# Memory's keys and values as 512-column products with a VectorE join, and the norms' transposes in the accumulating banks

## The reference, cut to what matters

```
def _memory_attention(q, mem, w_kv):                 # w_kv: 1024 x 512, one per layer
    km, vm = jnp.split(mem @ w_kv, 2, axis=-1)       # keys and values, 256 tokens x 256 each
    ...
    logits = jnp.einsum('bshd,bmhd->bhsm', q, km)
    probs = jax.nn.softmax(logits, axis=-1)
    return jnp.einsum('bhsm,bmhd->bshd', probs, vm)

for layer in range(DEPTH):
    p = x @ w_in                                     # mixer's inputs and memory's queries
    y = concatenate([mixed, recalled]) @ w_o[layer]
    x = _layer_norm(ALPHA * x + y, ...)
    x = _layer_norm(ALPHA * x + _conv_ffn(x, ...), ...)
```

## Time and profile before

| | |
|---|---|
| median of 3 runs | 1253.87 us (1253.64 to 1254.35) |
| span of the profiled execution, first to last instruction | 1251.8 us |
| TensorE busy, its mean granted clock | 1242.1 us (99%), 0.998 |
| VectorE busy | 1023.4 us (82%) |
| ScalarE busy | 729.7 us (58%) |
| KM products, 3 x 64 | L766, L767, L768 on memory |
| VM products, 3 x 64 | L791, L793, L795 on memory |

### The profile page before, as it was taken

The page is one execution under the profiler, slowest core; times in us unless marked ns, Lnnn a source line. Parts: engine busy times, 40 slices in busy tenths (PEclk is TensorE's granted clock), DMA queues, the critical chain, the costliest instruction groups (busy, mean ns, idle before and its releaser), DMA issues.

```text
span 1251.8 us, 19743 instructions
## 1 busy us (share of the span) xinstructions
PE 1242.1 (99%) x7408; PEld 1088.8 (87%) x7408; DVE 1023.4 (82%) x1596; ACT 729.7 (58%) x1187; POOL 20.0 (2%) x29
## 2 busy tenths in 40 slices
PE   8999999999999999999999999999999999999997
PEld 7898888888999998888888888888888888888886
DVE  5776888888879888988888878988888776888887
ACT  5666665555676545655554545655554674755552
POOL 0000000000000000000000000000000000000000
PEclk9999999999999999999999999999999999999999
DMA  9634475555453345666655665665555533666561
GB/s 329 223 120 146 169 249 182 189 188 193 161 184 122 129 140 167 220 202 188 192 189 170 211 209 172 221 200 187 190 193 171 187 118 119 212 209 202 191 193 54
DMA packets 63530, 228.23 MB, mean 182 GB/s; under 512 B 7462, under 2 KB 9126, under 8 KB 62412
## 3 DMA queue, kind: packets, MB, share of 16 engines
q1 hardware_dynamic: 63436, 226.97, 55.1%
HBM read 225.88 MB, written 1.06 MB: 181 GB/s over the span
## 4 chain that ended last, share of the span: by engine, by line
PE 99%; DVE 0%; issue 0%; DVEq 0%
PE pair L734 28%; PE acc L828 21%; PE pair L737 14%; PE pair L766 4%; PE pair L767 4%; PE pair L768 4%; PE acc L734 2%; PE acc L809 2%; PE acc L807 2%; PE acc L808 2%; PE pair L996 2%; PE pair L791 1%; PE pair L795 1%; PE pair L793 1%; PE acc L907 1%; PE acc L737 1%
## 5 line engine op out<-in xcount | busy, mean ns | idle before, releaser
L1253 DVE TENSOR_TENSOR w_lo<-raw,w_hi 128x1024 fp32r<-128x1024 f32 x403 | 485.9, 1220 | 109.8 <-ACT w_hi L1019 108.3
L1019 ACT ACTIVATE w_hi<-raw 128x1024 fp32r<-128x1024 f32 x403 | 423.7, 1058 | 213.7 <-PE pair L737 71.6
L734 PE MATMUL pair<-xT,w_hi 128*128 128x512 f32 x1520 | 478.0, 396 | 0.0
L737 PEld LDWEIGHTS pair<-xT,w_lo 128*128 128x128 f32 x1520 | 285.5, 188 | 67.1
L737 PE MATMUL pair<-xT,w_lo 128*128 128x256 f32 x1520 | 298.7, 278 | 0.0
L734 PEld LDWEIGHTS pair<-xT,w_hi 128*128 128x128 f32 x1520 | 233.8, 189 | 3.1 <-issue 0.3
L1066 ACT ACTIVATE hid<-pair 128x512 f32<-128x512 f32 x88 | 52.6, 597 | 126.0 <-PE pair L737 126.0
L766 PE MATMUL pair<-xT,w_hi 128*128 128x256 f32 x352 | 102.5, 291 | 0.0
L1294 DVE TENSOR_TENSOR hid<-pair,hid 128x512 f32<-128x512 f32 x88 | 60.6, 689 | 48.0 <-ACT hid L1066 47.6
L767 PE MATMUL pair<-xT,w_hi 128*128 128x256 f32 x352 | 99.5, 283 | 0.0
L768 PE MATMUL pair<-xT,w_lo 128*128 128x256 f32 x352 | 99.5, 283 | 0.0
(11 more groups left out here) (219 smaller groups left out, 1668.5 us busy)
## 6 DMA issues: line engine op xcount, KB each, us to landing
raw<-in_stream SPq DMA_DIRECT2D x404, 512.0 KB, 4.6
gains<-in_ln SPq DMA_DIRECT2D x8, 1024.0 KB, 8.5
bias<-bias_scratch SPq DMA_DIRECT2D x2, 1152.0 KB, 9.1
y_tok<-in_mem SPq DMA_DIRECT2D x1, 1024.0 KB, 11.1
out<-x_tok SPq DMA_DIRECT2D x4, 256.0 KB, 2.0
x_tok<-in_x SPq DMA_DIRECT2D x1, 512.0 KB, 3.7
x_tok<-in_x SPq DMA_DIRECT2D x2, 256.0 KB, 4.9
masks_in<-in_masks_c SPq DMA_DIRECT2D x1, 512.0 KB, 8.4
```

The lines of the kernel that those rows point to most:

```text
L734: pe.matmul(bank, w_hi[:, slot, kk * P:(kk + 1) * P], xT[:, kk].rearrange("p a s -> p (a s)"), start=(kk == 0), stop=(kk == KT - 1), skip_ ...
L737: last = pe.matmul(bank[:, 0:SEQ], w_lo[:, slot, kk * P:(kk + 1) * P], xT[:, kk, 0, :], start=False, stop=(kk == KT - 1), skip_group_check ...
L1019: nc.scalar.activation(w_hi[:, u % SPLIT, :], raw[:, u % RAW, :], ACT.Copy).then_inc(hi_ready, 1)
L1253: v.tensor_tensor(w_lo[:, u % SPLIT, :], raw[:, u % RAW, :], w_hi[:, u % SPLIT, :].bitcast(F32), ALU.subtract).then_inc(lo_ready, 1)
```

## The change

1. KM becomes wide: it reads the memory in one tile `memT` with the parts side by side, as x has it, and uses both banks of its pair. The "begun" first half of its second unit, used in the close, moves to the wide code.
2. VM becomes wide with the roles exchanged: memory is the weight, and 512 columns are the high and the low part of the streamed weights. These now lie in one tile `w_split`, high and low part of a slot one after the other. Two k of 512-column products are followed by two of 256.
3. ScalarE copies the upper halves (`mem_lower`), VectorE adds the lower ones (`join`) and only then are keys or values ready. The join is pending work like the taps: it stands behind the first half of the next chunk. Pending work is now put ahead of a chunk's `between` items.
4. All transposes of norms go to ACC: tile 0 to ACC 0 and 1, tile 1 to ACC 2 and 3.

```
-    LATER = {"UA": "taps", "UB": "taps"}
+    LATER = {"UA": "taps", "UB": "taps", "KM": "join", "VM": "join"}
...
         items.append(("half", c, 0))
         if levels:
             round_early(2 * c + 1 + AHEAD)
-        items.extend(between)
         items.extend(late)
         late.clear()
+        items.extend(between)
...
             if following:
 
+                late.append(("join", c + 1))
                 chunks.append(following)
...
+    mem_wide = {c for c, ch in enumerate(chunks) if ch[1] in ("KM", "VM")}
...
-    EARLY_TURNS = {(m, 1) for m in range(2 * DEPTH - 1)}
+    EARLY_TURNS = {(m, t) for m in range(2 * DEPTH - 1) for t in range(TT)}
...
-                chunks[item[1]][1] in ("UA", "UB") or item[1] in xq_wide | qk_wide):
+                chunks[item[1]][1] in ("UA", "UB") or item[1] in xq_wide | qk_wide | mem_wide):
             banks = (proj_ord[item[1]] % 2,)
...
-        w_hi = sb("w_hi", [P, SPLIT, UNIT], F32R)
-        w_lo = sb("w_lo", [P, SPLIT, UNIT], F32R)
+        w_split = sb("w_split", [P, SPLIT, 2, UNIT], F32R)
+        w_hi, w_lo = w_split[:, :, 0, :], w_split[:, :, 1, :]
...
-            return ACC[b] if items[pos][1:3] in EARLY_TURNS else side_bank(pos, b)
+            return ACC[2 * items[pos][2] + b] if items[pos][1:3] in EARLY_TURNS else side_bank(pos, b)
...
-                elif role in ("UA", "UB") or c in conv_wide | xq_wide | qk_wide:
+                elif role in ("UA", "UB", "KM") or c in conv_wide | xq_wide | qk_wide:
...
+                    of = memT if role == "KM" else xT
+                    first, end = (0, KT // 2) if begun else (KT // 2 if i == 1 and c in parted else 0, KT)
+                    for k in range(first, end, 2):
...
+                elif role == "VM":
+
+                    if i == 0:
+                        side(pos)
+                    for t in [0] if begun else [1] if i == 1 and c in parted else [0, 1]:
+                        bank, tok = PAIR[proj_ord[c] % 2][:, t, :], slice(t * P, (t + 1) * P)
+                        for j in range(0, 4, 2):
+                            for jj in (j, j + 1):
+                                pe.matmul(bank.rearrange("p (a e) -> p a e", a=2), a_hi(4 * i + jj, tok),
+                                          w_split[:, slot, :, jj * 256:(jj + 1) * 256], start=(i == 0 and jj == 0), stop=(i == 1 and jj == 3),
+                                          skip_group_check=True)
+                            for jj in (j, j + 1):
+                                last = pe.matmul(bank[:, 0:256], a_lo(4 * i + jj, tok), w_hi[:, slot, jj * 256:(jj + 1) * 256],
+                                                 start=False, stop=(i == 1 and jj == 3), skip_group_check=True)
...
+                elif c in mem_wide:
+                    nc.scalar.activation(km[:] if role == "KM" else vm[:], PAIR[n % 2][:, :, SEQ:512], ACT.Copy).then_inc(mem_lower, 1)
...
+            def join(c):
+                to, ready = (km, km_ready) if chunks[c][1] == "KM" else (vm, vm_ready)
+                dve.wait_ge(mem_lower, sorted(mem_wide).index(c) + 1)
+                v.tensor_tensor(to[:], PAIR[proj_ord[c] % 2][:, :, 0:SEQ], to[:], ALU.add).then_inc(ready, 1)
```

More of the change, by code:

```diff
@@ L339, in trunk_kernel @@
         raw = sb("raw", [P, RAW, UNIT])
-        w_hi = sb("w_hi", [P, SPLIT, UNIT], F32R)
-        w_lo = sb("w_lo", [P, SPLIT, UNIT], F32R)
+        w_split = sb("w_split", [P, SPLIT, 2, UNIT], F32R)
+        w_hi, w_lo = w_split[:, :, 0, :], w_split[:, :, 1, :]
         xT = sb("xT", [P, KT, 2, SEQ], F32R)
         xT_hi, xT_lo = xT[:, :, 0, :], xT[:, :, 1, :]
-        memT_hi = sb("memT_hi", [P, KT, SEQ], F32R)
-        memT_lo = sb("memT_lo", [P, KT, SEQ], F32R)
+        memT = sb("memT", [P, KT, 2, SEQ], F32R)
+        memT_hi, memT_lo = memT[:, :, 0, :], memT[:, :, 1, :]
         mixT_hi = sb("mixT_hi", [P, KT, SEQ], F32R)
@@ L475, in trunk_kernel @@
         rows_done, rows_ready = sem("rows_done"), sem("rows_ready")
-        xq_lower, qk_lower = sem("xq_lower"), sem("qk_lower")
+        xq_lower, qk_lower, mem_lower = sem("xq_lower"), sem("qk_lower"), sem("mem_lower")
         xq_ready, km_ready, vm_ready = sem("xq_ready"), sem("km_ready"), sem("vm_ready")
@@ L728, in half @@
                             side(pos)
-                    for k in range(0, KT, 2):
-                        if i == 0 and k == KT // 2:
+                    of = memT if role == "KM" else xT
+                    first, end = (0, KT // 2) if begun else (KT // 2 if i == 1 and c in parted else 0, KT)
+                    for k in range(first, end, 2):
+                        if i == 0 and k == KT // 2 and role != "KM":
                             pe.wait_ge(turn_lo, xT_turned)
                         for kk in range(k, k + 2):
-                            pe.matmul(bank, w_hi[:, slot, kk * P:(kk + 1) * P], xT[:, kk].rearrange("p a s -> p (a s)"),
+                            pe.matmul(bank, w_hi[:, slot, kk * P:(kk + 1) * P], of[:, kk].rearrange("p a s -> p (a s)"),
                                       start=(kk == 0), stop=(kk == KT - 1), skip_group_check=True)
                         for kk in range(k, k + 2):
-                            last = pe.matmul(bank[:, 0:SEQ], w_lo[:, slot, kk * P:(kk + 1) * P], xT[:, kk, 0, :],
+                            last = pe.matmul(bank[:, 0:SEQ], w_lo[:, slot, kk * P:(kk + 1) * P], of[:, kk, 0, :],
                                              start=False, stop=(kk == KT - 1), skip_group_check=True)
@@ L760, in half @@
                     every = slice(0, SEQ)
-                    first, end = (0, KT // 2) if begun else (KT // 2 if i == 1 and c in parted else 0, KT)
-                    for k in range(first, end):
+                    for k in range(KT):
                         at = slice(k * P, (k + 1) * P)
-                        if i == 0 and k == KT // 2 and role != "KM":
+                        if i == 0 and k == KT // 2:
                             pe.wait_ge(turn_lo, xT_turned)
@@ L781, in half @@
                             last.then_inc(value_done, 1)
+                elif role == "VM":
[11 more added lines that the diff above has]
+                                                 start=False, stop=(i == 1 and jj == 3), skip_group_check=True)
                 elif form == "T":
                     bank = PROJ[proj_ord[c] % 2]
-                    for t in [0] if begun else [1] if i == 1 and c in parted else [0, 1]:
+                    for t in range(TT):
                         dst, tok = bank[:, t * 256:(t + 1) * 256], slice(t * P, (t + 1) * P)
@@ L1417, in _ @@
                     outer_taps(item[1])
+                elif name == "join":
+                    join(item[1])
                 elif name == "q0":
```

## The result

| | before | changed |
|---|---|---|
| median | 1253.91 us (1253.64 to 1254.35, 5 runs) | 1258.39 us (1258.26 to 1258.77, 5 runs) |
| ratio | | 1.0038, 95% interval 1.0027 to 1.0048 |
| span of the profiled execution | 1251.8 us | 1256.5 us |

The account below looks back on a forecast made before the run. TensorE, busy 1242.1 of 1251.8 us, was taken as the bound, with VectorE costing only where TensorE waits. Layer 0 +2.1 and six closes +2.1 gave +4.2 us: span 1256.0, median 1258.1; range 1254.5 to 1260.3.

Parts of the forecast that it names:

- Products, -11.5 ns per k: Keys and values chunks: wide products take 348 ns per k instead of 360; 1.5 us less over 128 units.
- Layer 0, bias rows, +0.78: Layer 0's keys chunk start: first product waits for ScalarE's copy of the bias rows from its bank; +0.78 us.
- Layer 0, memory logits and third query-key chunk, together with the bias rows +2.1: Layer 0: both wait for joins behind weight roundings; logits +1.32, chunk +2.12 us including the earlier delays.
- The idle times: Layer 0, changed profile: TensorE idle about 0.8 us before the memory logits and 0.8 before the third query-key chunk.
- Six closes, +2.1: Ends of half layers: TensorE waits for joins queued behind roundings; 0.34 us at three with keys, 0.36 at three with values.
- release read from one row: TensorE's start after a wait on VectorE: weight load 0.06 us after VectorE's end, part of 0.18 us per wait.
- TensorE would be there at 140.20: Close with keys: the FFN's second chunk could start at 140.20 with the 0.18 us gain, but the join allows 140.72.
- pure-gain rival: Closes and layer 0: joins end early enough, no wait comes, only -1.5 us remains, 1252.4; chance 7%.
- Transposes, 0: Norms: moving transposes to accumulating banks costs 0; bounds 0.1 us less or more for each of seven.
- Read across high and low parts, 0: Values' product: reading weight parts 4 KB apart costs 0; if a tenth slower, layer 0 pays 0.2 to 0.4 us.

Follow-up runs that it names:

- e2: Changed kernel with all eight joins one weight rounding earlier on VectorE and layer 0's bias rows in the other pair's side bank; 1253.26 us.
- e1: Changed kernel with all eight joins put one weight rounding earlier in VectorE's queue, nothing else different; 1254.29 us.
- e4: Changed kernel with only the six joins of the closes one rounding earlier, layer 0's two left in place; 1255.98 us.
- e6: Changed kernel with each of the eight joins computed twice, once more into a spare tile ahead of the real one; 1263.03 us.
- e9: e2 plus, after each close's memory chunk, the next chunk starting on rounded weights alone, waiting for subtracted ones only before its first 256-column product; 1251.88 us.
- e10: Control: the kernel before, with the same later wait for subtracted weights as e9 at its six closes; 1252.65 us.
- e3: Kernel before with only the norm transposes moved to the accumulating banks, keys and values still narrow; 1253.52 us.
- e5: Changed kernel with the transposes' move undone, the first token tile's going to the side banks again; 1299.80 us.
- e7: e2 with one weight rounding's subtraction per close moved from VectorE to GpSimd; 1261.34 us.
- e8: Control: the kernel before, with one weight rounding's subtraction at each of six closes on GpSimd; 1261.94 us.

## Why the prediction was right

- **Products, -11.5 ns per k:** right. Both chunks run at the wide form's pace, and layer 0 keeps 0.39 us once nothing waits (e2), where 2 x 0.18 was reckoned. The rule of the Trainium skill ("TensorE: Matmul & The Clock Gate", section "Back-to-back issue gap") would have given 0.08 us there, an estimate from that page. The page gives that rule for a single product on its own and says itself that a stream of products does not follow it, which the prediction did not say.
- **Layer 0, bias rows, +0.78:** right, 0.84 by e1 against e2.
- **Layer 0, memory logits and third query-key chunk, together with the bias rows +2.1:** right, 2.32, 0.2 more than forecast. By e1 the two joins' order costs 1.87 of it. The idle times, 0.80 and 0.77, are as forecast (0.8 each).
- **Six closes, +2.1:** right in size, 2.11, and in cause (e4: gone with the order; e6: +0.61 per 0.60 us of VectorE). Two details of the working were off and cancelled; that is luck. The join started 0.13 us earlier than by my count (four roundings before it take 4.64 us, and it overlaps with the last), and at that close the weight load came 0.23 us after its end (143.04 to 143.27), not 0.06; at the next close it was 0.11. A release read from one row is a weak term.
- **"TensorE would be there at 140.20":** wrong, without effect on the sum. The gain of the keys chunk ends at UA's start, which the rounding before it sets; only by e1 and e9 this came to light. The pure-gain rival of -1.5 us could therefore not have come true by moving the joins alone: with them early, and the bias rows away, it is -0.4 (e1, e2). It needed the later wait as well, and even then the wide form's own share, e9 against its control e10, is 1.1 us (0.36 in layer 0, 0.76 at the closes), not 1.5; the rest of what e9 gains, its control gains too.
- **Transposes, 0:** right alone (e3). I had named what they allow, not its price, 41 us (e5).
- **Read across high and low parts, 0:** right, 697 ns per two k in the values chunk too.

Not tested: keys wide and values narrow, or the other way round.

## What to carry to other kernels

When a sum of halves moves from "copied by one engine" to "copied, then added by another", look first at where it stands in the second engine's queue: here one place earlier made 4.1 of 4.5 us vanish, with the same work. A faster filling chunk gains nothing while the next chunk's start is set by another engine's chain; look at who ends last at *that* start before counting the gain. It is worth a look whether a wait for two operands can be split, so that the products which need only the early one go first (here 0.13 to 0.25 us at each of six places).

## What the hardware showed that I had not expected

- An elementwise instruction on GpSimd stops a VectorE instruction that reads two SBUF operands: 0.75 us became 2.79 while GpSimd ran its 2.37 us, at all six closes of e7 (together +7.7 us; +8.1 in e8). The Trainium skill, "SBUF — State Buffer", section "Terms", says that the two engines share a pair of ports by an exclusive lock for a whole instruction; the trace agrees.
- After a wait of 4.2 to 4.8 us on TensorE the granted clock stood at the lower of its two levels (e5: 0.53 from 134.9 to 138.5 us, 0.50 from 498.5 to 503.5). The stall cost 1.6 us more than its length at the first close and 2.4 at the third.
